# Moving a block's modulation ahead of its networks, and two down projections as seven products of halves

## The reference, cut to what matters

```
h = causal_depthwise_conv(xn @ w_up, conv_w) + conv_b
g, u = jnp.split(h, 2, axis=-1)
return (jax.nn.gelu(g) * u) @ w_down          # w_down: 2816 x 1024
```

```
mod  = silu_c  @ w_mod + b_mod                # w_mod: 1024 x 6144
modc = silu_cc @ w_mod + b_mod
```

## Time and profile before

| | us |
|---|---|
| median of 3 runs | 2530.83 (2528.49 to 2532.82) |
| the profiled execution's own time | 2534.89 |
| its span, first to last instruction | 2533.0 |
| TensorE busy | 2481.1, 98% of the span |
| VectorE busy | 1272.5, 50% |
| ScalarE, GpSimd busy | 542.8 (21%), 551.2 (22%) |
| read from HBM | 331.72 MB, 131 GB/s over the span |

### The profile page before, as it was taken

How to read it: one execution, slowest core, us unless ns; L and a number is a source line. 1 busy time by engine, 2 the same in 40 slices (tenths; PEclk the granted TensorE clock), 3 DMA queues, 4 the chain that set the end, 5 groups by cost and what they waited for, 6 DMA issues and landing times.

```text
span 2533.0 us, 36719 instructions
## 1 busy us (share of the span) xinstructions
PE 2481.1 (98%) x14004; PEld 2023.3 (80%) x14004; DVE 1272.5 (50%) x2606; ACT 542.8 (21%) x1193; POOL 551.2 (22%) x474
## 2 busy tenths in 40 slices
PE   9989999999999999999999999999999999999999
PEld 6857889986799998644567766888888875899999
DVE  4034168851325887323846763554551246435774
ACT  1131122112212220213630001222200215212220
POOL 1000135200212540001002321322241010232543
PEclk9999999999999999999999999999999999999999
DMA  6323264653334566120014562121222120244443
GB/s 234 133 100 116 83 223 177 250 197 133 115 135 167 191 224 232 67 92 27 1 77 146 218 245 113 67 99 66 112 92 80 67 94 26 101 158 158 166 191 109
DMA packets 39970, 334.59 MB, mean 132 GB/s; under 512 B 3872, under 2 KB 10144, under 8 KB 22688
## 3 DMA queue, kind: packets, MB, share of 16 engines
q1 hardware_dynamic: 39840, 332.78, 35.5%
HBM read 331.72 MB, written 1.05 MB: 131 GB/s over the span
## 4 chain that ended last, share of the span: by engine, by line
PE 92%; DVE 4%; DMA 2%; POOL 1%; issue 1%; ACT 1%; DVEq 0%; SPq 0%; POOLq 0%; ACTq 0%
PE PS L769 24%; PE PS L569 21%; PE PS L2756 7%; PE PS L1029 6%; PE PS L1529 5%; PE PS L1719 4%; PE PS L2797 4%; PE PS L1338 3%; PE PS L1704 3%; PE PS L2276 2%; PE PS L1349 2%; PE PS L1361 2%; PE PS L436 1%; DMA slot<-in_weights 1%; PE PS L750 1%; PE PS L2414 1%
## 5 line engine op out<-in xcount | busy, mean ns | idle before, releaser
L769 PE MATMUL PS<-SQ,slot 128*128 128x128 f32 (+1 forms) x1984 | 294.5, 301 | 3.7 <-DVE slot L865 3.7
L569 PE MATMUL PS<-XN,slot 128*128 128x256 f32 (+1 forms) x1184 | 296.8, 411 | 0.8 <-DVE XN L508 0.8
L769 PEld LDWEIGHTS PS<-SQ,slot 128*128 128x128 f32 x1984 | 268.1, 191 | 17.1 <-DVE slot L865 4.2
L569 PEld LDWEIGHTS PS<-XN,slot 128*128 128x128 f32 x1184 | 224.4, 190 | 69.9 <-issue 42.5
L769 PE MATMUL PS<-XN,slot 128*128 128x128 f32 (+1 forms) x1664 | 250.0, 301 | 0.0
L569 PE MATMUL PS<-arena,slot 128*128 128x256 f32 x1088 | 237.0, 379 | 1.6 <-DVE arena L1956 1.5
L769 PEld LDWEIGHTS PS<-XN,slot 128*128 128x128 f32 x1664 | 226.1, 192 | 10.7
L569 PEld LDWEIGHTS PS<-arena,slot 128*128 128x128 f32 x1088 | 206.2, 190 | 31.8 <-DVE arena L1956 2.3
L892 DVE SCALAR_TENSOR_TENSOR arena<-PS,small,arena 128x255 f32<-128x255 f32 (+2 forms) x352 | 174.8, 543 | 45.8 <-ACT arena L836 44.6
L836 ACT ACTIVATE arena<-PS,small 128x256 f32<-128x256 f32 (+1 forms) x176 | 105.3, 616 | 380.1 <-DVE PS L925 244.0
L480 POOL TENSOR_TENSOR SQ<-SQ 128x512 f32<-128x512 f32 (+1 forms) x36 | 42.4, 1184 | 540.5 <-ACT SQ L446 539.9
(11 more groups left out here) (289 smaller groups left out, 3669.6 us busy)
## 6 DMA issues: line engine op xcount, KB each, us to landing
slot<-in_weights SPq DMA_DIRECT2D x85, 2048.0 KB, 7.8
arena<-in_mod SPq DMA_DIRECT2D x96, 512.0 KB, 3.6
slot<-in_weights SPq DMA_DIRECT2D x16, 2816.0 KB, 9.8
slot<-in_weights SPq DMA_DIRECT2D x24, 1536.0 KB, 6.8
slot<-in_weights SPq DMA_DIRECT2D x5, 1024.0 KB, 4.8
slot<-in_weights SPq DMA_DIRECT2D x2, 2176.0 KB, 8.8
arena<-in_c SPq DMA_DIRECT2D x3, 1024.0 KB, 10.4
small<-in_small SPq DMA_DIRECT2D x1, 1982.0 KB, 17.7
```

The source lines that it names most:

```text
L569: mm = pe.matmul(o, l, r, start=k == 0, stop=k == len(terms) - 1, skip_group_check=True)
L769: mm = pe.matmul(PS[:, bank, 0:h], lhs[:, k * P:(k + 1) * P], rhs(k), start=first and k == 0, stop=last and k == 3, skip_group_check=True)
```

## The change

The networks a0 and a1 now call `tensor_down_seven` and its companions as b1 does; with no gate, the result is added to X. In a1 the norm of the context, which stood beside the first job, now stands between the first and the second pair (`then`).

All 48 modulation tiles are computed before a0 begins. VectorE does tiles 0 to 6 after the start of the program's scalars, 7 to 17 among the reads of foxin, 18 to 23 after them, 24 to 29 among the reads of mixout0, 30 to 39 between the norm before xq0 and the cross attention xatt0, and 40 to 47 among the reads of xo0. c is loaded and put through Silu twice: into the second half of X behind slab 2, and into the area at 12288 in mixout0. There are two slots for the loads instead of four. SP issues after slab g the tiles that the list gives (4 after slab 3, 3 after slab 4, and so on), each from the third on after a wait for the second product of the tile two before it.

The core of the diff:

```diff
-        MODC = H[:, 0:DK, T:2 * T].rearrange("p (g j) t -> p g j t", g=2)
-        MODP = H[:, DK:DK + 4, T:2 * T]
-        mod_slots = [area(15360 + D * i, 4, T) for i in range(4)]
+        MODC = [X[:, :, T:2 * T].rearrange("p (g j) t -> p g j t", g=2), area(12288, 2, 4, T)]
+        mod_slots = [area(16384 + D * i, 4, T) for i in range(2)]
+        MODP = area(18432, 4, T)
...
+        MOD_LOADS = {g: [] for g in range(len(table))}
+        for g, n in zip((3, 4, 5, 6, 7, 8, 9, 10, 12, 13, 14, 15, 16, 17, 18), (4, 3, 3, 3, 3, 3, 3, 2, 4, 4, 2, 3, 4, 6, 1)):
+            done = sum(len(v) for v in MOD_LOADS.values())
+            MOD_LOADS[g] = list(range(done, done + n))
...
+        def vector_mod_tiles(dve, *tiles):
+            for n in tiles:
+                w = mod_slots[n % 2]
+                c = MODC[n // MOD_HALF]
+                if n % MOD_HALF == 0:
+                    dve.wait_ge(*of("silu_c", n // MOD_HALF))
+                dve.wait_ge(sems[f"mod_landed{n % 2}"], 16 * (n // 2 + 1))
+                for g in range(2):
+                    if g == 0 and n:
+                        dve.wait_ge(*of("mod_tile", n - 1, 0))
+                    vector_mod_product(dve, w, c[:, g, :, :], MOD[:, 0, n, g:g + 1], w if g else MODP)\
+                        .then_inc(*tick(VD, "mod_tile", n, g))
+                if n % MOD_HALF == MOD_HALF - 1:
+                    vector_mod_end(dve, 0, n // MOD_HALF, [("mod_tile", n, 1)])
+
+        def scalar_silu_c(act, f):
+            act.wait_ge(sems["loaded_c"], 16 * (f + 1))
+            act.activation(MODC[f], MODC[f], ACT.Silu).then_inc(*tick(SD, "silu_c", f))
...
+                if then and p == 0:
+                    then(pe)
...
+            add(tensor=lambda pe: tensor_down_seven(pe, s, DK // 2, n, tensor_then),
+                vector=lambda d: vector_down_seven(d, s, DK // 2, n, gate, vector_then),
+                gpsimd=lambda p: gpsimd_down_seven(p, s, DK // 2, n))
...
                 add(scalar=scalar_start, vector=vector_start, tensor=tensor_start)
+                add(scalar=lambda a: scalar_silu_c(a, 0), vector=lambda d: vector_mod_tiles(d, *range(0, 7)))
...
+                def vector_foxin(dve, jobs=fox_jobs):
+                    for j, job in enumerate(jobs):
+                        vector_mod_tiles(dve, *{2: range(7, 12), 3: (12,), 6: range(13, 18)}.get(j, ()))
+                        reads_linear(dve, VD, "vector", "foxin", [job], j)
+                    vector_mod_tiles(dve, *range(18, MOD_HALF))
...
+                        [(24, 25), (26, 27), (28, 29), ()])
...
+                add(vector=lambda d: vector_mod_tiles(d, *range(30, 40)))
                 add_linear("xq0", q_jobs)
...
+                        [(40, 41), (42, 43), (44, 45), (46, 47)])
...
+            def load_mod(n):
+                if n >= 2:
+                    sp.wait_ge(*of("mod_tile", n - 2, 1))
+                sp.dma_start(mod_slots[n % 2], mod_in[n].rearrange("p (j t) -> p j t", t=T))\
+                    .then_inc(sems[f"mod_landed{n % 2}"], 16)
...
+                if g == 2:
+                    load_c(0)
+                if g == first_slab["mixout0"] + 1:
+                    sp.wait_ge(*of("subln", "out", 3, 0))
+                    load_c(1)
+                for n in MOD_LOADS[g]:
+                    load_mod(n)
```

More of the change, by code:

```diff
@@ L605, in conv_spec @@
             return n, taps, centre
[L608 to L616, removed]
+        MOD_HALF = MOD_TILES // 2
+        MOD_LOADS = {g: [] for g in range(len(table))}
@@ L1610, in add_ffn @@
             n = T * len(segs)
-            early = block == "b"
             add(tensor=lambda pe: tensor_up_seven(pe, s, norm, segs), scalar=lambda a: scalar_up_seven(a, s, segs),
                 vector=lambda d: vector_up_seven(d, s, norm, segs),
-                gpsimd=lambda p: gpsimd_up_seven(p, s, n, (lambda e: gpsimd_down_sums(e, s, 0)) if early else None))
-            if block == "a":
-                add(vector=lambda d: [vector_mod_tile(d, s, r, g) for r in range(5, 11) for g in range(2)])
+                gpsimd=lambda p: gpsimd_up_seven(p, s, n, lambda e: gpsimd_down_sums(e, s, 0)))
+            tensor_then = vector_then = None
             if aside:
@@ L1627, in add_ffn @@
                 return
[L1628 to L1636, removed]
@@ L1638, in add_out @@
-        def add_out(s, rhs, ready, k_tiles, segs, gate=None, needs=None, then=None, mod=None):
-            def reads(j, bank):
[L1641 to L1653, removed]
-                return out
-            jobs = feature_jobs(rhs, ready or (lambda k: None), DK, reads, k_tiles=k_tiles, segs=segs)
-            if then:
-                jobs[0]["then"] = then
-            if needs:
-                jobs[0]["needs"] = {(0, k): [needs(k)] for k in (0, FM - 2, FM - 1)}
-                jobs[0]["needs"] = {i: [l for l in ls] for i, ls in jobs[0]["needs"].items()}
-            if mod is None:
-                add_linear(s, jobs)
-                return
@@ L2213, in two_blocks @@
             if l == 0:
[L2214 removed]
+                add_out("xo0", lambda k: O1[:, k, :], lambda k: ("xatt0", "out", k // 2), DK, [0],
+                        [(40, 41), (42, 43), (44, 45), (46, 47)])
                 units = norm_x(s, X, XN, lambda m, g: col("ffn_norm0", m), after_out("xo0", [0], None), [0])
@@ L2226, in two_blocks @@
                 if l == 1 else None)
-            prev_ready = after_out(f"da{l}", [0], None)
+            prev_ready = [[(f"da{l}", "read", 2 * p, 1)] for p in range(DK // 2)]
         add_norm("final", norm_x("final", X, X, lambda m, g: col("final_norm", m), prev_ready, [0]))
```

103 lines of the change are left out of this document (29 added, 74 removed).

## The result

The changed kernel takes 2549.99 us (median of 4 runs, 2548.45 to 2552.32), the kernel before 2531.64 beside it: ratio 1.0074, 95% interval 1.006 to 1.0088, 18.4 us slower. Predicted were 2546, with a range of 2533 to 2560. The profiled execution took 2552.32 us; its span is 17.5 us longer than that of before.

A forecast was written before the change was run, and what follows sets the result against it. TensorE, busy in 98% of the span, was taken as the bound. New waits and slower clock lose 28.9 us, 13.3 are gained: +15.6 from 2530.83 gives 2546 us, range 2533 to 2560 (the forecast's own 2540 to 2554).

The forecast's parts named there:

- pause at slab 4: Before foxin, slab 4's load waits in SP's queue behind the products of tiles 0 and 1; TensorE pauses 15.6 us.
- norm behind mixout0: After mixout0, job 2 is read late behind modulation tiles, so the norm's matmul comes late; 2.1 us added.
- from the norm to xatt0 (slabs 14 and 15): Slab 14 waits behind tiles 30 and 31, 0.2 us; in xq0, slab 15 is issued behind tile 33, 3.1 us.
- xatt0, first minimum: Cross attention: tiles 30 to 39 stand on VectorE ahead of its first minimum, so TensorE waits; 6.1 us added.
- up projections a0, a1: Products, the load of c and Silu leave the loops of networks a0 and a1; 2.1 + 1.1 = 3.2 us gained.
- da0: Down projection of a0 in seven products, taking 70.95 us as db1 does, instead of 76.0; 5.0 us gained.
- da1: Down projection of a1 in seven products at db1's 70.95 us, the context's norm beside it; 5.0 us gained.
- rival 3: Slab 4 is not late; the gain stays, with 0 to 5 us of attention lost: 2517 to 2523 us, chance 0.05.
- rival 2: Weights and tiles together bound the kernel; at 20% slower transfers +32 us, 2563 us, chance 0.15.
- I add that 1.8 once: TensorE's clock falls to half after the long pause before foxin; 1.8 us lost, counted one time only.
- rival 1: Loads do not queue behind each other: 18.6 lost against 13.3 gained, +5.3 us, 2536 us, chance 0.17.
- Rival 4: Slab 4 late, gains nearly at their bounds (18.2 us), later steps half: +5 us, chance 0.05.

The follow-up runs named there:

- e1: Changed kernel without layer 0's modulation: the 48 tiles' loads and 96 products left out, two memsets in place of the sums; 2522.15 us, ratio 0.9963.
- e2: Changed kernel with all 96 products kept but only tiles 0 and 1 loaded, later products reading those again; 2523.43 us, ratio 0.9969.
- e3: Changed kernel with the loads of tiles 0 to 23 placed differently among the slabs in SyncE's queue, none behind slab 4; 2536.68 us, ratio 1.0025.
- e6: Changed kernel with the loads of tiles 0 to 23 issued by GpSimd instead of SyncE, same order and waits; 2553.43 us, ratio 1.0082.
- e4: Changed kernel with GpSimd's three sums for the context's norm waiting for VectorE's sum s4 of the first pair; 2548.50 us, ratio 1.0067.

## Why the prediction was right, and where its sizes were off

| step | predicted, us | measured, us |
|---|---|---|
| pause at slab 4 | 15.6 | 15.5 |
| clock after it | 1.8 | 2.0 |
| norm behind mixout0 | 2.1 | 3.6 |
| from the norm to xatt0 (slabs 14 and 15) | 0.2 + 3.1 | 5.6 |
| xatt0, first minimum | 6.1 | 4.2 |
| xo0 | 0 | -0.2 |
| lost | 28.9 | 30.7 |
| up projections a0, a1 | 3.2 | 1.7 + 0.5 |
| da0 | 5.0 | 5.3 |
| da1 | 5.0 | 1.9 |
| gained | 13.3 | 9.4 |

The measured column is the length of each stage, from start to start, after against before; the pause is 86.08 - 67.03 against 72.89 - 69.34.

- **Slab 4** failed in nothing: order, path and size are in the chain above, and e1 to e3 show that it is SyncE's queue, and so does e6, where the slabs have that queue to themselves and foxin starts on time beside the same loads. The prediction's rival 3 (slab 4 on time) falls with it, and its rival 2 (bandwidth): in foxin no slab after the fourth is late. One sum ahead of rival 2 does not come out: at 20% slower transfers SP's cycle is 13.5 to 13.9 us, not 14.6, so hardly a slab of foxin would be late. The forecast does not rest on it.
- **"I add that 1.8 once"** is the step that was mis-sized among the losses. The clock fell after all four pauses. The norm's six records took 2.47 us for 1.46, which is 1.0, and xq0's second half 15.74 where half of the 27.86 in the earlier trace rows is 13.9, which is 1.8: with the wait of 2.67 these make 5.5 of the 5.6. The Trainium skill, "TensorE: Matmul & The Clock Gate", section "What's actually happening", calls the throttled clock the default that activity releases, which the prediction noted and did not count; the trace agrees, with 0.50 behind each of the four pauses.
- **The norm** came 1.5 us later than worked out: c landed 0.7 us behind its due time, and one product, beside GpSimd's first sum, took 2.24 us instead of 1.23.
- **xatt0** went the way described, VectorE coming to the first minimum out of the products; due 2.03 us after xatt0's start by the earlier trace rows, so at 302.34, the minimum came at 306.47, 4.1 late instead of 6.1. TensorE had lost 2.3 us more ahead of it than worked out (5.6 for 3.3), about the difference; the two errors nearly cancel (9.8 for 9.4 together), which is luck.
- The prediction's rival 1 (loads don't queue) gave nothing lost at the norm and at xatt0; both lost. Its pause, 14.4, was also too short. Rival 4 (gains near their bounds, later steps half) falls with gains of 9.4 where it had 18.2.
- **da1** is the gain that failed: the prediction took db1's row for both, and of the norm beside it looked only at pair 1. The price came in pair 0, before the norm's matmul, where GpSimd's sums meet VectorE's. e4 shows it: 3.3 us, of which 2.7 are the two waits and the rest the clock behind them. The Trainium skill, "GPSIMD Engine Reference", section "Key points", names contention of the two engines' interfaces for VectorE instructions with two SBUF inputs, which these sums have; the trace agrees, with 1.61 against 2.69 us on the one side and 1.26 against 2.65 on the other.
- **The up projections** gave 2.2 of 3.2: a1 was already near the pace of the changed loop.

So the loss between the gates and the end of da1 is 30.7 - 9.4 = 21.3 us, where 15.6 was forecast; the profiled spans differ by 17.5, as this execution reached the gates 2.3 us earlier than that of before and was 1.5 shorter behind da1 (the gains of 10.9 us in the expectations are the 9.4 and this 1.5). The medians differ by 18.4. So the terms were 5.7 us too favourable, losses and gains together, and the medians show only 2.8 of it.

## What to carry to other kernels

Before a load is put into a queue that also feeds the bound engine, list what stands behind it and when each of those slots comes free: a wait for a product holds all of them, and DMA engines that are idle for most of the span (their share is 34.9% here) say nothing about that. Bytes and side work that cost 30 us in one order cost nothing in another, with two slots more from tile 23 on, so the order is worth planning from the traces' own times, with the attention's end where it is and not where a plan puts it. A duration read off one place holds elsewhere only if the same engines are at work beside it.

## What the runs showed of the hardware that was not expected

VectorE's and GpSimd's additions of two SBUF operands hold each other up: 128x1408 from 1.61 to 2.69 us, 128x512 from 1.26 to 2.65, 128x256 from 0.72 to 1.99. By the rows at 251 and 515 us the one that starts first keeps its length and the other waits for it; no run varied the order of a pair alone. And two 512 KB loads issued by GpSimd beside a 2048 KB load of SyncE landed after 7.9 us, against a median of 3.3 for those that SyncE issued in the same run, and the slab after 10.8 instead of 7.8; a separate queue is no priority.
